# The rounds of an RWKV-7 scan: how TensorE waits, how it turns 64x64 blocks, and in which order four engines take their steps

## Chip, cores and metric

One core of a Trainium2 chip runs the whole program. The metric is the device time of one execution in microseconds (us). Engines are named PE (TensorE), ACT (ScalarE), DVE (VectorE), POOL (GpSimd) and SP (SyncE).

## The reference

Two blocks of a network run one after the other on 256 tokens (and 256 context tokens) of width 1024. The change touches one piece of the first block, the RWKV-7 scan with 16 heads of 64:

```
# rwkv7_scan: S (heads, 64, 64), one step for each token
sa = S @ (-kk_t)
S  = S * w_t + outer(sa, kk_t * a_t) + outer(v_t, k_t)
y_t = S @ r_t
```

It runs forward and backward in time. In each direction the context's tokens are scanned from a zero state, where only the last state is of use, and then the 256 latent tokens, whose outputs y are read.

## The kernel before

`rwkv_scan_stage` computes the scan in chunks of 64 tokens. The two directions are two **lanes**, 0 and 1, with tiles of their own. A **round** takes one chunk for 8 of the 16 heads, in both lanes. There are 16 rounds: 0 to 7 only write the state (`RW_READS` is 8), 8 to 15 also read outputs. In a round each lane solves a 64x64 triangular system for each head by doubling, in six levels. All of it is fp32. A product of 64x64 blocks is one call and two matmul records in the trace, so a step of 8 calls is 16 records ("x16").

The steps, with the lines that issue them on PE:

- `CT`, `LK` (`cross`, L3241, 16 records each) and `CC` (`cross_both`, L3250, moving 128 columns): the tables of the next round, from alpha, beta, kappa and the state. In read rounds `RKB` (L3241, 32 records) makes two tables with rho.
- `Y2` to `Y6` and `E2` to `E6` (`cross_late`, L3258, 16 records each): the levels. `D1` to `D5` turn the matrix `e` for them. In rounds 0 to 7 a turn is a product with the identity inside 64x64 tiles of the array (`turn_by_product`, L3241, 16 records); in rounds 8 to 15 it is two 128x128 transposes (`turn`, L3269, 2 records).
- `V` and `KB` turn v, kappa and beta, by 128x128 transposes in every round (2 and 4 records).
- `U`, `LKV`, `R` (`own`, L3264, 16 records), `S` and `O` (`cross` of two products, 32 records): update, state and outputs. A `'` in the order means the step of the round before, a `+` one of the round after.

One level of one lane is a chain over three engines: `Y` and `D` on PE, ACT copies both out of PSUM (L3384, L3391), `E` on PE, and DVE merges it into `e` (L3489), which the next `Y` reads.

`rwkv_order` gives each engine its own list of steps for a round. PE's instructions stand in two loops (`Fori`), of 8 and of 7 passes; round 15 stands behind them, unrolled. The other engines' instructions are unrolled. Since PE's loop body is the same in each pass, it waits against a register that grows by one in each pass, and adds one to a second semaphore:

```
def wait(e, lane, step):                                  # L3280
    pe.wait_ge(sig.sems[e, lane, step].sem, at)
    if not isinstance(at, int):
        pe.sem_inc(carried.sem, 1)
```

PE's order in rounds 0 to 7 is Y2 D1 U' of both lanes, E2 S', Y3 D2, V KB, E3 LKV, Y4 D3, E4, Y5 D4, E5, each for lane 0 and then lane 1; then Y6 D5 CT+ CC+ LK+ of lane 0, the same of lane 1, E6 E6. Rounds 8 to 15 add R behind D1, O' behind S' and RKB behind D3.

Of the kernel before, what the change touches and what calls it, by code (L numbers as in the profile page):

```python
# [3029 lines left out]

def rwkv_order(engine, n):

    late, read, more = n >= 1, n >= RW_READS, n + 1 < RW_ROUNDS
    inside = 0 <= n < RW_ROUNDS

    def lane(d, *steps):  # L3040
        at = {"'": n - 1, "+": n + 1}
        return [(d, s.rstrip("'+"), at.get(s[-1], n)) for s in steps]

    def both(*steps):
        return [x for d in LANES for x in lane(d, *steps)]

    fore = [lane(d, "CT+", "CC+", "LK+") if more else [] for d in LANES]
    reads, behind, kept = ["RKB"] * read, ["O'"] if n > RW_READS else [], ["S'"] if more else []
    if engine == "pe":
        if n < 0:  # L3050
            return fore[0] + fore[1]
        if read:
            behind = ["O'"]
        if not inside:
            return both("U'", *behind)
        return [*both("Y2", "D1", *["R"] * read, "U'"), *both("E2", *kept, *behind), *both("Y3", "D2"), *both("V", "KB"), *both("E3", "LKV"), *both("Y4", "D3", *reads), *both("E4"),
                *both("Y5", "D4"), *both("E5"), *lane(0, "Y6", "D5"), *fore[0], *lane(1, "Y6", "D5"), *fore[1], *both("E6")]
    if engine == "act":
        scales = both("shrink+", "grow+") if more else []
        if n < 0:  # L3060
            return scales
        behind = ["U'"]
        if not inside:
            return both(*behind)
        return [*both("Y2", "D1", *behind), *scales, *both("Y3", "D2"), *both("KB"), *both("Y4", "D3"), *both("Y5", "D4"), *both("Y6", "D5")]
    if engine == "dve":
        last = lane(0, "last+") + lane(1, "last+") if more else []
        if n < 0:
            return fore[0] + fore[1] + last
        if not inside:  # L3070
            return both(*behind)
        return [*both("copy"), *both("E2", *kept, *behind), *both("E3", "LKV"), *both(*reads), *both("E4"), *both("E5"), *fore[0], *fore[1], *both("E6"), *last]
    if n == RW_ROUNDS:
        return []
    ahead = [*both("ident+"), *both("alpha+"), *(both("scale'") if late and more else []), *both("state+", "vn+"), *both("beta+", "kappa+")] if more else []
    return [*ahead, *(both("rho+") if more and n + 1 >= RW_READS else []), *both(*["R"] * (read and inside))]


class ScanSignals:
# [3 lines left out]
    LAG = {"U": 1, "S": 1, "O": 1, "E6": 1, "kappa": -1}  # L3083
    STEPS = {"act": ("D1", "D2", "D3", "D4", "D5", "U", "KB", "grow", "shrink"),
             "dve": ("CC", "LK", "E2", "E3", "E4", "E5", "E6", "S", "O", "LKV", "RKB", "last", "copy"),
             "pool": ("alpha", "kappa", "rho", "scale", "R")}

    def __init__(self, core):
        self.sems = {(e, lane, s): core.counter(f"rw_{e}_{s}_{lane}") for e, steps in self.STEPS.items() for lane in LANES for s in steps}
        self.level = max(c.base for c in self.sems.values()) + 1  # L3090
        self.pe = [core.counter(f"rw_pe_steps_{lane}") for lane in LANES]
        self.pe_at, self.pe_n = {}, 0
        for n in range(-1, RW_ROUNDS + 1):
            for d, step, m in rwkv_order("pe", n):
                if d == 0:
                    self.pe_n += 1
                    self.pe_at[step, m] = self.pe_n

    def value(self, step, m):
        return self.level + m + 1 + self.LAG.get(step, 0)  # L3100

    def first(self, step):
        return RW_READS if step in ("R", "RKB", "rho", "O") else -1 if step in ("U", "S") else 0

    def align(self, eng):

        for (e, lane, s), c in self.sems.items():
            by = self.value(s, self.first(s) - 1) - c.base
            if by:
                eng.sem_inc(c.sem, by)  # L3110

    def wait_pe(self, eng, lane, step, m):
        eng.wait_ge(self.pe[lane].sem, self.pe[lane].at(self.pe_at[step, m]))

    def wait(self, eng, e, lane, step, m):
        eng.wait_ge(self.sems[e, lane, step].sem, self.value(step, m))

    def done(self, ins, e, lane, step, m):
        if (e, lane, step) not in self.sems:
            return  # L3120
        c = self.sems[e, lane, step]
        ins.then_inc(c.sem, 1)
        c.n = self.value(step, m) - c.base

    def settle(self):
        for c in self.pe:
            c.n += self.pe_n


def rwkv_scan_stage(core, st, rw):  # L3130
# [12 lines left out]
    with ExitStack() as ctx, core.engines_block() as block:  # L3143
# [16 lines left out]
        names = ("shrink", "kappa", "alpha", "rho", "e1", "e", "y", "d", "lk", "w", "vn", "store0", "store1")  # L3160
# [3 lines left out]
        for d in LANES:  # L3164
            sources, turned, rkb = (host[:, d * share + a * N * C:d * share + b * N * C].rearrange("p (x n t) -> p x n t", n=N, t=C) for a, b in ((0, 2), (2, 5), (5, 7)))
            cw = core.sb(f"cw_{d}", [P, N, 2, C], ctx=ctx)[:]
            ur = core.sb(f"ur_{d}", [P, 2, N, C], ctx=ctx)[:]
# [2134 lines left out]
```

## Time and profile before

| what | us |
|---|---|
| median of 3 runs | 3288.19 (3282.24 to 3291.73) |
| profiled execution | 3287.64, its span 3285.9 |
| scan stage, from POOL's first memset to the next stage's first matmul | 1056.2 to 1395.2 of the span |
| PE busy over the span | 3040.2 (93%) |
| mean granted clock of PE | 0.957 of 2.4 GHz |

The span runs from the first to the last instruction; the profiled execution's time is 1.7 us longer than it. Times in the rows are microseconds from the start of the span. Rows of one engine in a timeline overlap because matmuls are pipelined and their ends are modelled, so the cost of a step in a stream is the distance from its start to the start of the next. "PEclk" is the share of 2.4 GHz that PE was granted, and a row with "issue" is idle time in which PE waited for nothing that the profile shows.

### The profile page before, as it was taken

How to read it: one execution, taken by the hardware profiler on the slowest of the kernel's cores; microseconds unless marked ns; L12 is line 12 of the kernel's file. 1: busy time of each engine (PE TensorE's matmuls, PEld its weight loads, DVE VectorE, ACT ScalarE, POOL GpSimd, SP SyncE). 2: the span in 40 equal slices, each digit the busy share in tenths (PEclk: the TensorE clock that was granted, in tenths of full speed). 3: DMA queues.
4: the chain of work that ended last, by engine and by line, in shares of the span. 5: the costliest groups of instructions: out<-in, count | busy, mean ns of one | idle time of the engine just before them, and what ended most of it. 6: DMA issues, size and time to landing. Idle time of an engine off the chain costs nothing. (4 is left out here: it accounts for less than half of the span.)

```text
span 3285.9 us, 68297 instructions
## 1 busy us (share of the span) xinstructions
PE 3040.2 (93%) x27176; PEld 2492.1 (76%) x27176; DVE 2371.4 (72%) x3483; ACT 1743.1 (53%) x2797; POOL 615.4 (19%) x720
## 2 busy tenths in 40 slices
PE   5998889999797888879999999998999999999998
PEld 4774568878673777759986998866788888888887
DVE  5868754468847444477866778545799999999998
ACT  2424433232314443335445534765788888888887
POOL 0007124321100434318423111331000000000000
PEclk8998999999898999989989999998999999999999
DMA  6536224446211000048652798402899999999997
GB/s 221 170 108 20 103 84 153 141 147 207 96 58 26 1 1 1 2 171 271 253 161 65 275 328 302 140 27 79 320 370 367 371 369 366 373 366 368 370 360 261
DMA packets 337306, 646.56 MB, mean 197 GB/s; under 512 B 23853, under 2 KB 144281, under 8 KB 337113
## 3 DMA queue, kind: packets, MB, share of 16 engines
q1 hardware_dynamic: 316233, 568.38, 51.0%
q0 software_dynamic: 20160, 73.41, 6.1%
q8 instruction: 117, 1.92, 0.2%
q10 hardware_dynamic: 720, 2.23, 0.2%
q14 instruction: 76, 0.62, 0.1%
HBM read 641.34 MB, written 1.05 MB: 196 GB/s over the span
## 5 line engine op out<-in xcount | busy, mean ns | idle before, releaser
L5095 DVE TENSOR_TENSOR weights_lo<-raw_ring,weights_hi 128x1024 fp32r<-128x1024 f32 x336 | 400.8, 1220 | 35.6 <-ACT weights_hi L5025 28.4
L5025 ACT ACTIVATE weights_hi<-raw_ring 128x1024 fp32r<-128x1024 f32 x336 | 356.7, 1065 | 89.4 <-PE bank_pair L4961 53.2
L5095 DVE TENSOR_TENSOR weights_lo<-H,weights_hi 128x1024 fp32r<-128x1024 f32 x224 | 268.6, 1221 | 25.1 <-ACT weights_hi L5025 18.2
L4961 PE MATMUL bank_pair<-weights_hi,expert_x_hi 128*128 128x512 f32 x896 | 281.7, 396 | 4.9 <-DVE weights_lo L5095 4.8
L4961 PE MATMUL bank_pair<-weights_hi,expert_x_lo 128*128 128x512 f32 x896 | 277.2, 391 | 0.0
L4961 PE MATMUL bank_pair<-weights_lo,expert_x_hi 128*128 128x512 f32 x896 | 276.8, 390 | 0.0
L5025 ACT ACTIVATE weights_hi<-H 128x1024 fp32r<-128x1024 f32 x224 | 236.5, 1060 | 58.5 <-PE bank_pair L4961 43.2
L2715 DVE SCALAR_TENSOR_TENSOR conv<-bank_pair,vec,conv 128x189 f32<-128x189 f32 (+3 forms) x396 | 138.5, 427 | 146.0 <-ACT conv L2675 146.0
L4961 PEld LDWEIGHTS bank_pair<-weights_lo,expert_x_hi 128*128 128x128 f32 x896 | 168.5, 188 | 36.1
L4961 PEld LDWEIGHTS bank_pair<-weights_hi,expert_x_lo 128*128 128x128 f32 x896 | 168.5, 188 | 36.0
L4961 PEld LDWEIGHTS bank_pair<-weights_hi,expert_x_hi 128*128 128x128 f32 x896 | 163.8, 189 | 36.2 <-issue 5.1
L1349 PE MATMUL bank_pair<-Y_parts,const_parts 128*128 128x256 f32 (+1 forms) x592 | 145.7, 331 | 1.6 <-DVE H_parts L1394 1.6
L4973 PE MATMUL bank_pair<-weights_hi,hidden_hi 128*128 128x512 f32 x448 | 138.7, 391 | 0.0
L4973 PE MATMUL bank_pair<-weights_hi,hidden_lo 128*128 128x512 f32 x448 | 138.0, 389 | 0.0
L4973 PE MATMUL bank_pair<-weights_lo,hidden_hi 128*128 128x512 f32 x448 | 138.0, 389 | 0.0
L5095 DVE TENSOR_TENSOR weights_lo<-const,weights_hi 128x1024 fp32r<-128x1024 f32 x112 | 134.0, 1219 | 3.5
L5025 ACT ACTIVATE weights_hi<-const 128x1024 fp32r<-128x1024 f32 x112 | 119.4, 1066 | 31.9 <-PE bank_pair L4961 21.6
L629 DVE SCALAR_TENSOR_TENSOR mod_sums_ada<-mod_ring_ada,act,mod_sums_ada 128x1024 f32<-128x1024 f32 x84 | 115.4, 1379 | 4.8 <-DMA mod_ring_ada<-in_w_ada 4.8
L1349 PEld LDWEIGHTS bank_pair<-Y_parts,const_parts 128*128 128x128 f32 x592 | 101.9, 191 | 14.0 <-DVE const_parts L1329 2.4
L1138 PE MATMUL bank_pair<-const 128*128 128x512 f32 (+1 forms) x140 | 75.3, 649 | 32.2 <-PEq L214 32.2
L3384 ACT ACTIVATE const<-bank_pair 128x128 f32<-128x128 f32 x80 | 22.5, 282 | 150.3 <-PE bank_pair L3269 80.7
L1349 PE MATMUL bank_pair<-H_parts,const_parts 128*128 128x256 f32 (+1 forms) x296 | 97.7, 330 | 0.0
(802 smaller groups left out, 8366.9 us busy)
## 6 DMA issues: line engine op xcount, KB each, us to landing
raw_ring<-in_moe_w_gate SPq DMA_DIRECT2D x64, 1024.0 KB, 6.2
raw_ring<-in_moe_w_up SPq DMA_DIRECT2D x56, 1024.0 KB, 7.0
ring_up<-in_ffn_w_up SPq DMA_DIRECT2D x110, 512.0 KB, 4.0
H<-in_moe_w_down SPq DMA_DIRECT2D x48, 1024.0 KB, 5.1
raw_ring<-in_moe_w_down SPq DMA_DIRECT2D x48, 1024.0 KB, 5.1
mod_ring_ada<-in_w_ada POOLq DMA_DIRECT2D x84, 512.0 KB, 6.3
ring_down<-in_ffn_w_down SPq DMA_DIRECT2D x66, 512.0 KB, 6.0
H<-in_moe_w_gate SPq DMA_DIRECT2D x32, 1024.0 KB, 7.2
```

What stands on the lines that cost most here:

```text
L629: ins = self.core.nc.vector.scalar_tensor_tensor(total, tile, scale, total, ALU.mult, ALU.add)
L1138: core.nc.tensor.matmul(core.bank(bank)[:, cols], st.C("ones"), st.const[:, cols], start=True, stop=True)
L1349: ins = self.core.nc.tensor.matmul(self.bank(it, o)[:, 0:T], w, y, start=s == self.begin[o] and k == 0 and a == 0, stop=s == self.end[o] a ...
L2715: ins = nc.vector.scalar_tensor_tensor(out, shifted, tap(w, 2 * it + o), out, ALU.mult, ALU.add)
L3384: nc.scalar.activation(by_slot(t["y"])[:, :, :, 0:C // 2], Y[d], ACT.Copy)
L4961: ins = nc.tensor.matmul(bank, x[:, k * SEATS:(k + 1) * SEATS].bitcast(F32R), w[:, j * WIDE:(j + 1) * WIDE], start=k == 0 and i == 0, stop ...
L4973: ins = nc.tensor.matmul(DOWN[half], x, w[:, half * 512:(half + 1) * 512], start=c == 0 and i == 0, stop=c == FEC - 1 and i == 2)
L5025: nc.scalar.activation(hi[:, u % CUTS].bitcast(F32R), raw_part(u), ACT.Copy).then_inc(cut.sem, 1)
L5095: nc.vector.tensor_tensor(lo[:, u % CUTS].bitcast(F32R), raw_part(u), hi[:, u % CUTS], ALU.subtract).then_inc(parted.sem, 1)
```

## The change

1. **Waits.** Most semaphores that PE waits for become tokens: the producer adds one, PE waits for the constant 1 (`take`), and the second call of the step takes one away again (`then_inc(..., -1)`). Only `V`'s wait for `S` keeps its register. Six steps of a round (`Y2`, `CT`, `CC` of both lanes) take two tokens.
2. **Turns.** A turn is made inside 64x64 tiles: for s = 0 a transpose, for s = 1 a product with the identity, 12 records by the count of calls. It is used for D1 to D5 in every round, and for V and KB in rounds 0 to 7. In rounds 8 to 15 V and KB keep the 128x128 transposes.
3. **Tables.** alpha and rho stand side by side (`keys`), and `CT` and `LK` are `cross_both` products with both, 128 moving columns each, in every round; `RKB` goes. DVE masks the rho halves with two instructions (`RB`, `RK`) into `fresh`, and copies both to `rkb` later (`cp`).
4. **Order.** Lists written out by hand for four engines, one for write and one for read rounds.

```diff
+RW_STEPS = {
+    ("pe", False): "Y20 U0' D10 Y21 U1' D11 E20 S0' S1' E21 Y30 V0 D20 KB0 Y31 D21 E30 V1 KB1 E31 Y40 D30 LKV0 Y41 D31 LKV1 E40 E41 CT0+ Y50 D40 LK0+ Y51 D41 E50 CT1+ LK1+ E51 Y60 D50 CC0+ Y61 D51 E60 CC1+ E61",
+    ("act", False): "grow0+ shrink0+ U0' D10 U1' D11 grow1+ shrink1+ D20 D21 KB0 KB1 D30 D31 D40 D41 D50 D51",
+    ("dve", False): "copy1 copy0 E20 S0' E21 S1' E30 E31 LKV0 E40 last0+ last1+ E41 LKV1 CT0+ E50 LK0+ E51 CT1+ LK1+ CC0+ E60 CC1+ E61",
+    ("pool", False): "alpha0+ alpha1+ scale1' vn0+ beta0+ scale0' ident0+ kappa0+ vn1+ state1+ beta1+ ident1+ kappa1+ state0+",
+    ("pe", True): "Y20 R0 D10 U0' Y21 D11 R1 E20 U1' E21 S0' O0' S1' Y30 D20 Y31 O1' D21 E30 V0 KB0 V1 KB1 E31 LKV0 Y40 D30 Y41 D31 LKV1 E40 CT0+ E41 LK0+ Y50 D40 Y51 D41 CT1+ E50 LK1+ E51 Y60 D50 CC0+ Y61 D51 E60 E61 CC1+",
+    ("act", True): "grow0+ D10 U0' D11 shrink0+ U1' grow1+ shrink1+ D20 D21 KB0 KB1 D30 D31 D40 D41 D50 D51",
+    ("dve", True): "copy1 copy0 E21 E20 O0' S0' O1' S1' E30 E31 last0+ LKV0 cp0 LKV1 E40 cp1 E41 CT0+ RB0+ LK0+ RK0+ E50 CT1+ E51 RB1+ LK1+ RK1+ CC0+ E60 E61 last1+ CC1+",
+    ("pool", True): "R0 alpha1+ alpha0+ rho1+ scale0' rho0+ beta0+ beta1+ ident0+ kappa0+ vn0+ state0+ ident1+ kappa1+ scale1' vn1+ R1 state1+",
+}
...
+    def take(self, eng, e, lane, step):
+        c = self.tokens[e, lane, step]
+        eng.wait_ge(c.sem, c.base + 1)
+        return c.sem
...
-            def turn_by_product(out, x):
-                return cross(out, [(x, ident)])
+            def turn(out, x):
+                for j in (0, 1):
+                    for s in (0, 1):
+                        for r in (0, 1):
+                            head, unit = x[HALF[r], 2 * j + s], st.C("pair_ident")[HALF[r]]
+                            if s:
+                                ins = nc.tensor.matmul(out[HALF[s], r, j], head, unit, start=True, stop=True)
+                            else:
+                                ins = nc.tensor.transpose(out[HALF[s], r, j], head, unit)
+                return ins
...
+                    def first(ins):
+                        count[0] += 1
+                        if count[0] > 1 and taken:
+                            ins.then_inc(taken.pop(0), -1)
...
                     if step == "CT":
-                        wait("pool", d, "kappa")
+                        take("pool", "kappa")
                         if n >= 0:
-                            wait("dve", d, "RKB" if n >= RW_READS else "LKV")
-                        ins = cross(SLOT0[d], [(t["beta"], t["alpha"])])
+                            take("dve", "LKV")
+                        ins = cross_both(WIDE0[d], t["beta"], t["keys"], first)
+                    elif step == "LK":
+                        ins = cross_both(WIDE1[d], t["kappa"], t["keys"], first)
                     elif step == "CC":
-                        ins = cross_both(WIDE[d], t["alpha"], t["sources"])
+                        take("pool", "state")
+                        take("dve", "LK")
+                        ins = cross_both(WIDE1[d], t["alpha"], t["sources"], first)
...
                     elif kind == "D":
-                        ins = (turn if n >= RW_READS else turn_by_product)(TURN[d], t["e1" if l == 1 else "e"])
+                        ins = turn(TURN[d], t["e1" if l == 1 else "e"])
...
-                        cross(SLOT0[d], [(t["kappa"], t["rho"])])
-                        ins = cross(SLOT1[d], [(t["beta"], t["rho"])])
...
                     elif step == "R":
-                        sig.wait(pool, "act", d, "U", m - 1)
+                        sig.wait_pe(pool, d, "O", m - 1)
...
+                    elif step in ("RB", "RK"):
+                        mask = st.C(f"upto_{d}").unsqueeze(1).unsqueeze(1).to_broadcast([P, 2, 2, C])
+                        if m > RW_READS:
+                            sig.wait(dve, "dve", d, "cp", m - 1)
+                        wide_slot, i = (WIDE0, 1) if step == "RB" else (WIDE1, 0)
+                        ins = nc.vector.tensor_tensor(by_slot(t["fresh"][:, i]), wide_slot[d][:, :, :, 1], mask, ALU.mult)
+                    elif step == "cp":
+                        ins = nc.vector.tensor_copy(t["rkb"], t["fresh"])
```

## Rows read from the trace of the kernel before

**Rows 1.** The windows view, seven rounds of the scan: length, busy time of each engine, granted clock
```profile
1065.60:1086.70 21.10, 16.55 (x732) 14.93 (x724) 8.48 (x25) 8.03 (x28) 6.13 (x12) 1.00 0.02 4
1137.80:1154.90 17.10, 14.96 (x719) 14.03 (x716) 8.17 (x26) 8.05 (x28) 7.20 (x14) 1.00 0.00 0
1206.20:1236.10 29.90, 24.61 (x736) 21.34 (x736) 9.72 (x28) 8.71 (x28) 9.94 (x18) 0.77 0.01 3
1236.10:1258.80 22.70, 20.59 (x736) 18.06 (x736) 9.60 (x29) 8.67 (x28) 9.90 (x18) 0.92 0.00 0
1280.50:1302.20 21.70, 19.19 (x740) 16.81 (x736) 10.05 (x30) 8.67 (x28) 9.89 (x18) 1.00 0.00 1
1302.20:1326.80 24.60, 22.10 (x740) 19.34 (x736) 10.02 (x29) 8.71 (x28) 9.90 (x18) 0.86 0.00 0
1348.50:1371.60 23.10, 20.59 (x740) 18.04 (x736) 10.00 (x29) 8.66 (x28) 9.90 (x18) 0.93 0.00 0
```

**Rows 2.** The view of TensorE's register waits, line 3280, over the span
```profile
L3280 PEldq EVENT_SEMAPHORE  x552: 51/51/51, 1065.1 to 1371.0; - x184
```

**Rows 3.** The timeline of TensorE in one write round: start, length, group, idle before it
```profile
1139.33 0.43 PE L3258 MATMUL bank_pair<-const,cw 64*64 64x32 f32 x16 [1.49 <-DVE const L3489]
...
1149.12 0.43 PE L3258 MATMUL bank_pair<-const,cw 64*64 64x32 f32 x16
1149.34 0.47 PE L3241 MATMUL bank_pair<-const 64*64 64x64 f32 x16
1149.60 0.42 PE L3258 MATMUL bank_pair<-Y,cw 64*64 64x32 f32 x16
...
1150.48 0.44 PE L3258 MATMUL bank_pair<-const 64*64 64x32 f32 x16 [0.20 <-ACT const L3391]
...
1151.46 0.43 PE L3258 MATMUL bank_pair<-const,cw 64*64 64x32 f32 x16
...
1151.94 0.44 PE L3241 MATMUL bank_pair<-const,H 64*64 64x64 f32 x16
1152.17 0.65 PE L3250 MATMUL bank_pair<-H,const 64*64 64x128 f32 x16
1152.61 0.44 PE L3241 MATMUL bank_pair<-const 64*64 64x64 f32 x16
```

**Rows 4.** The timeline of TensorE in one read round
```profile
1282.39 0.44 PE L3269 MATMUL bank_pair<-const 128*128 128x128 f32 x2
1282.76 0.68 PE L3264 MATMUL bank_pair<-const,H 64*64 64x64 f32 x16
1283.28 0.57 PE L3264 MATMUL bank_pair<-const 64*64 64x64 f32 x13
...
1283.71 0.41 PE L3258 MATMUL bank_pair<-Y,cw 64*64 64x32 f32 x14
...
1290.13 0.38 PE L3269 MATMUL bank_pair<-const,H 128*128 128x128 f32 x2
1290.45 0.43 PE L3258 MATMUL bank_pair<-const 64*64 64x32 f32 x16
```

**Rows 5.** The timeline of ScalarE and TensorE: a register wait released, write round
```profile
1147.66 0.30 ACT L3391 ACTIVATE const<-bank_pair 128x128 f32<-128x128 f32 x1
...
1148.10 0.43 PE L3258 MATMUL bank_pair<-const 64*64 64x32 f32 x16 [0.20 <-ACT const L3391]
```

**Rows 6.** The same in the last round, which waits on a constant
```profile
1387.95 0.27 ACT L3391 ACTIVATE H<-bank_pair 128x128 f32<-128x128 f32 x1
...
1388.28 0.43 PE L3258 MATMUL bank_pair<-Y,H 64*64 64x32 f32 x16 [0.17 <-ACT H L3391]
```

**Rows 7.** The timeline of TensorE in the expert stage: four transposes and what follows
```profile
2585.14 0.60 PE L4932 MATMUL bank_pair<-const 128*128 128x128 f32 x4
2585.50 0.71 PE L4961 MATMUL bank_pair<-weights_hi,expert_x_hi 128*128 128x512 f32 x2
```

**Rows 8.** Groups by line and shape, VectorE in the scan stage: busy, mean ns, idle before
```profile
L3507 DVE TENSOR_TENSOR H<-bank_pair,const 128x512 f32<-128x512 f32 x16 | 11.1, 691 | 12.2 <-PE bank_pair L3241 12.2
```

More of the change, by code:

```diff
@@ L3028 @@
 LANES = (0, 1)
-def rwkv_order(engine, n):
[L3037 to L3076, printed above, removed]
@@ new lines @@
+RW_STEPS = {
[8 rows of a table added]
+}
+def rwkv_order(engine, n):
+    read, more = n >= RW_READS, n + 1 < RW_ROUNDS
+    steps = []
+    for word in RW_STEPS[engine, read].split():
+        step, d, at = step_of(word)
+        ahead, behind = at == "+", at == "'"
+        if (ahead and not more) or (not ahead and n < 0) or (not behind and n == RW_ROUNDS):
+            continue
+        if (step == "S" and not more) or (step == "scale" and not (n >= 1 and more)) or (step == "O" and engine == "dve" and n == RW_READS):
+            continue
+        first_read = n == RW_READS - 1
+        if first_read and engine == "pool" and step == "kappa":
+            steps.append((d, "rho", n + 1))
+        steps.append((d, step, n + ahead - behind))
+        if first_read and engine == "dve" and step in ("CT", "LK"):
+            steps.append((d, "RB" if step == "CT" else "RK", n + 1))
+    return steps
@@ L3079, with step_of @@
+def step_of(word):
+    at = word[-1] if word[-1] in "+'" else ""
+    word = word.rstrip("+'")
+    return word[:-1], int(word[-1]), at
 class ScanSignals:
[L3083 to L3086, printed above, removed]
+    STEPS = {"act": ("grow", "shrink"), "dve": ("S", "O", "last", "copy", "CT", "cp"), "pool": ("scale", "R")}
+    TOKENS = {"act": ("D1", "D2", "D3", "D4", "D5", "U", "KB"), "dve": ("E2", "E3", "E4", "E5", "E6", "LKV", "LK", "CC"), "pool": ("kappa", "state")}
@@ L3112, in wait_pe @@
[L3112 to L3127, printed above, removed]
+                self.pe_n[d] += 1
@@ L3159, in tile @@
             return t.rearrange("p (n t) -> p n t", n=N)
-        names = ("shrink", "kappa", "alpha", "rho", "e1", "e", "y", "d", "lk", "w", "vn", "store0", "store1")
+        names = ("shrink", "kappa", "e1", "e", "y", "d", "lk", "w", "vn", "store0", "store1")
         T = [{n: tile(f"{n}_{d}") for n in names} for d in LANES]
@@ L3232, in _, with cross @@
         def _(pe):
-            ident = st.C("pair_ident").unsqueeze(1).to_broadcast([P, N, C])
-            def cross(out, products):
+            def cross(out, products, first=lambda ins: None):
                 for j in (0, 1):
@@ new lines, in rounds_from @@
+                            if not isinstance(at, int):
+                                pe.sem_inc(carried.sem, 1)
+                                carried.n += times
+                        else:
+                            pe.wait_ge(sig.sems["dve", d, "O"].sem, sig.value("dve", d, "O", n - 1))
+                        ins = (turn_whole if n >= RW_READS else turn)(SLOT2[d], t["vn"])
+                    elif step == "KB":
+                        by = turn_whole if n >= RW_READS else turn
+                        by(SLOT0[d], t["kappa"])
+                        ins = by(SLOT1[d], t["beta"])
+                    else:
+                        take("act", "KB")
+                        ins = own(SLOT0[d], t["lk"], t["vt"], first)
```

164 lines of the change are left out of this document (81 added, 83 removed).

## The prediction

> **What bounds the kernel now.** I read the page first: PE is busy 93% of the span, but the change touches one stage of 339 us, so only that stretch counts. Then the windows view by rounds, where the reader is to see four things. A write round takes 17.1 us at the full clock and a read round 21.7. Rounds 9, 12 and 14 are read rounds too and take 22.7, 24.6 and 23.1, with granted clocks of 0.92, 0.86 and 0.93; round 8 takes 29.9 at 0.77. Round 0 takes 21.1 at full clock. DVE, ACT and POOL stay at or under 10.1 of 21.7 us [rows 1]. So PE's sequence sets the length, as busy time and as waits for a chain that comes back to PE. Next the timeline of PE. Each pass of a loop starts with 1.49 us of idle PE. In a level without other work, level 5 of lane 0 starts at 1149.12 and level 6 at 1151.46: 2.34 us, while PE's six steps in between need 1.4, and the gap stands ahead of E5, which waits for ACT [rows 3]. PE executes 552 register waits of 51 ns each, some 37 in a pass [rows 2].
>
> **Prices of the steps on PE**, start to start. Y .22 ahead of a turn (I take .21 for Y and E); a turn by products .26; CT .23, CC with 128 moving columns .44 [rows 3]. R is .52 behind a 128x128 turn, U .43, so .47 for an own step; S and O are two crosses, .47. A 128x128 turn takes .37, and Y in front of it another .36 to .37 in place of .22, so going in and out of the full array costs some .25 a turn. Two full transposes with the way out cost .32 [rows 4], four without one .36 [rows 7]; so the 12 of V and KB are 1.1 to 1.3, with .3 for in and out.
> Write round before: 20 Y and E 4.2, 10 D 2.6, six own or double steps 2.8, V and KB 1.6, CT and LK .95, CC .9: 13.05. Add 1.49 idle and .2 for refilling PE at the loop's head; the other 2.35 are waits of the levels' chains. Read round before: 4.2, D 3.7 and 1.5 for the changes, ten own or double steps 4.7, V and KB 1.6, CT, LK, RKB and CC 2.8: 18.5. With the head 1.7 that leaves 1.5 of waits.
>
> **The edits.**
> *Turns.* A new turn has 12 records against 16 of the product. Nearest rows: 12/16 of CT's .23, that is .17, from below; above, a full turn with its changes of tile each time, .51. The two tiles that hold products still issue as many records each as in CT, so I take .24. V and KB in write rounds are six such turns, 1.45 against 1.6. The open question is whether a transpose among products empties the array. In the expert stage four transposes stand between products in one tile shape: start to start .36 for the four, under .1 each, so nothing is paid between the last of them and the product behind it [rows 7]. The cost in [rows 4] then belongs to the change of tile, which the new turn never makes. The Trainium skill says the same of the change (TensorEngine Tiling (Array Packing), Tiling Modes: changing the tiling mode drains the engine). It also speaks against this edit: by its Restrictions, column tiling excludes transpose mode for fp32. By the rows the turn is .24 or less; by that rule it would be a product, .26, some .3 us more in a round.
> *Tables.* CT and LK rise from .23 to .44. In write rounds this is work for nothing: 4 x .21 = +.84. In read rounds it replaces RKB: 4 x .44 against 4 x .23 and two times .47, -.1. DVE's masks go from 2 x .69 to more, smaller ones, and `cp` is new: a copy of 128x512, between nothing and the .69 of a mask of that size [rows 8]. DVE then has about 11.5 of 18 us, so it is covered by PE.
> *Waits.* A register wait released by ACT at 1147.96 lets PE start at 1148.10, .14 later [rows 3, 5]. In the last round, which waits on constants, ACT ends at 1388.22 and PE starts at 1388.28: .06 [rows 6]. So .08 for each exposed wait, and one event less at the loop's head, .15 by two such waits. The 34 taken tokens in a round each add a decrement to a matmul; no row shows its price, bounded by 0 and the 51 ns of an event [rows 2]. I take 0: a step that ends in an increment is followed at the same distance as any.
> *Order.* In levels 4 to 6 CT, LK and CC of both lanes now stand between E and Y, or Y and E. A level has .84 for Y and D of both lanes, .42 for E and .88 of tables, 2.2 in all, against a chain of 2.34 that loses two waits of .08 and is 2.2. PE is then bound by its own steps, and of 2.4 us of waits I keep .4. What is late next is POOL. In read rounds R0, which waits for O0', heads its list, and alpha, rho, beta and kappa for the next round are queued behind it. O0' ends about 4.1 us into the round; POOL's instructions take 9.89/18 = .55 [rows 1], kappa0 is the tenth and ends at 9.6; CT0 comes up at 10.1 on PE. This is .5 us of cover; I keep .8 of waits in a read round.
> *Prologue.* Two more memsets and another order on POOL: between 0 and 1 us, I take +1. The loops stay, so the head's idle time and round 0's extra do.
>
> **Sum.** Write round after: Y, E 4.2; D 2.4; own and double 2.8; V, KB 1.45; tables 6 x .44 = 2.65; head 1.55; waits .4: 15.45, so -1.65. Read round: 4.2, 2.4, 4.7, V and KB still on the full array 1.6, 2.65, 1.55, .8 = 17.9; against 21.7 I take -3.7. Eight of each: -13 and -29 (the last read round has no tables and gains less). The falls of the clock cost 1.0 + 2.9 + 1.4 in rounds 9, 12 and 14, and 5.2 in round 8 once 3 us of stalls of its first pass are taken off, 10.5 in all. They come only where D is a full turn [rows 1]; I take half back, -5. In all -13 - 29 - 5 + 1 = -46. The profiled execution took 3287.64 and the median is 0.55 above it, so both lead to 3242.
>
> **Rivals.**
> A, the other side: the transpose inside 64x64 tiles empties the array as a full turn does, .51 a turn. Sixteen turns in a write round and ten in a read round, 208 in all, at +.27: +56, so 3298. It decides from .46 a turn. For it: every full turn next to a 64x64 step pays. Against it: [rows 7]. .07.
> B: the clock also falls in write rounds. Transposes stand near all falls of the scan and products near none. A fall of one granted stretch costs 1.0 to 1.4; one in each round is +20 against the forecast: 3262. .12. The Trainium skill has such a rule (TensorE: Matmul & The Clock Gate, Part 4: transposes do not count as work for the clock in the same way).
> C: POOL is late. If the chain behind R0 ends 2 us later than I work out, CT0 stands for 1.5 in each read round: +12, 3254. .10.
> D: the decrements are not free. At 26 ns, half of an event's 51, 34 in a round are .9 us: +14, 3256. .06. The Trainium skill gives 26.3 ns for each increment that serializes (TensorE: Matmul & The Clock Gate, Part 3), which is near that half.
> E: the waits don't shrink, because the order only moves them, so that only the turns, the tables and a third of the clock come through: write rounds gain nothing, read rounds 2.5 each, -20 -3.5 +1: 3265. .07.
> My forecast has .58.
>
> **Range and chances.** 3228 to 3266. The low end is all of the clock back (-5.5), no waits in a round (-9): 3227. The high end takes in B to E one at a time. Faster by over 0.3% (9.9 us, about what a measurement here can tell from no change): forecast, B, C, D and E, less what an unknown stall could take: .88. Within 0.3%: .05, slower .07, nearly all from A.
>
> **What would show it.** Windows over a write round 15.2 to 15.7 long with PE idle only at its head, 1.3 to 1.4 us; a read round 17.5 to 18.5. D's start to the next step's .22 to .26 in all rounds; over .4 is A. A row with PE waiting for POOL's kappa is C. A granted clock of 1.00 in write rounds and above 0.95 in rounds 8 to 14; below that is B. Steps of 16 records at more than .22 with no wait named are D. The forecast is wrong if the level's period in the write rounds stays at 2.3.

## The result, and the profile after

The changed kernel took 3355.28 us (median of 4 runs, 3335.48 to 3357.55), the kernel before 3289.96 (4 runs beside it, 3282.24 to 3295.8): ratio 1.0187, interval 1.0142 to 1.0231. It is slower. The forecast was 3242 with a range of 3228 to 3266, so both the sign and the range were wrong.

The profiled execution took 3355.53 us. Its scan stage runs from 1056.1 to 1463.3 us of the span, 407.2 us in place of 339.0: the stage holds the whole difference. Up to the first branch of the loop (start of the stage and round 0) it takes 40.5 us in place of 30.1; rounds 1 to 7 together 181.6 in place of 119.5; rounds 8 to 14 160.5 in place of 165.5; the last one 24.6 in place of 23.8. So the write rounds lose 62 us, round 0 10, and the read rounds gain 5.

The windows view of the kernel after, one round to a row but for the last row (columns as in [rows 1]): write rounds 2 and 3, read rounds 10 and 11, and then the half-clock stretch inside round 2.

```profile
1121.10:1150.70 29.60, 29.39 (x747) 23.95 (x744) 8.23 (x24) 8.27 (x30) 7.11 (x14) 0.77 0.00 0
1150.70:1175.20 24.50, 24.30 (x748) 20.03 (x748) 8.16 (x25) 8.31 (x30) 7.06 (x14) 1.00 0.00 0
1324.10:1347.00 22.90, 22.56 (x785) 19.64 (x781) 11.31 (x32) 8.62 (x28) 10.02 (x18) 1.00 0.00 0
1347.00:1370.00 23.00, 22.66 (x787) 19.71 (x783) 11.34 (x33) 8.62 (x28) 10.02 (x18) 1.00 0.00 1
...
1130.30:1144.00 13.70, 13.70 (x238) 10.91 (x238) 2.22 (x8) 2.89 (x8) 4.75 (x10) 0.50 0.00 1
```

Read the first number against PE's busy time. In the write round of 24.5 us PE is busy for 24.3; in [rows 1] it was 14.96 of 17.10. The waits are gone, as the change meant, and yet the round is 7.4 us longer, with hardly more matmul records (748 against 719). More time for the same number of records is the signature of a dearer record, not of a wait. The first row adds a second, smaller loss: 13.7 us at a granted clock of 0.50, 1.2 GHz, make one round 5.1 us longer. There are three such stretches, in rounds 0, 2 and 6: some 15 us together, if the one in round 0 costs as much as the other two.

The view of waits says the same of the whole stage (us in total, times, longest). First the kernel before, PE over 1056 to 1395 us, then the kernel after, 1056 to 1463:

```profile
PE bank_pair L3258 <- DVE const L3489: 27.6, 23, 1.5
PE bank_pair L3241 <- POOL const L3419: 10.9, 1, 10.9
```

```profile
PE bank_pair L3248 <- POOL const L3425: 9.9, 1, 9.9
PE bank_pair L3257 <- ACT Y L3397: 3.1, 9, 0.3
PE bank_pair L3257 <- issue: 1.7, 8, 0.2
PE bank_pair L3257 <- DVE const L3494: 0.8, 2, 0.5
```

27.6 us of waits for VectorE's merge became .8. The largest wait left is that for POOL at the stage's start, which both have.

Where the time went is in the timeline of PE in a write round of the kernel after. L3281 is the new turn's transpose, L3279 its product; the cost of a step is again the distance to the next start.

```profile
1187.12 0.25 PE L3281 MATMUL bank_pair<-const,H 64*64 64x64 f32 x2
1187.29 0.33 PE L3279 MATMUL bank_pair<-const,H 64*64 64x64 f32 x4
1187.56 0.25 PE L3281 MATMUL bank_pair<-const,H 64*64 64x64 f32 x2
1187.73 0.27 PE L3279 MATMUL bank_pair<-const,H 64*64 64x64 f32 x2
...
1188.43 0.25 PE L3281 MATMUL bank_pair<-const 64*64 64x64 f32 x2
1188.61 0.33 PE L3279 MATMUL bank_pair<-const 64*64 64x64 f32 x4
1188.87 0.24 PE L3281 MATMUL bank_pair<-const 64*64 64x64 f32 x2
1189.05 0.28 PE L3279 MATMUL bank_pair<-const 64*64 64x64 f32 x2
```

Two transposes take .17 to .18, the two products behind them (x4) .26 to .27, and this twice: .88 us a turn, against .24 in the forecast and .26 for a turn by products [rows 3]. The four products of a turn all write the same half of the tiles, that is two tiles of the four. An `own` step also uses two tiles only, and its 16 records take .43 to .52 [rows 4] where those of a cross, in four tiles, take .23 [rows 3]. By that measure four records in two tiles cost some .12; here they cost .26. The tile shape (64*64) never changes. A passage between transpose and product, in either direction, seems to cost some .15, and the new turn makes four of them, since its innermost loops put two transposes, two products, two transposes, two products in a row. That was the theory that the experiments had to test.

### The profile page after: what moved, and what is told of

It is laid out like the page before. It is cut to its first block and busy times, and to the rows that moved or that the text cites. A ratio compares the mean times of both kernels' runs of the same rounds, so it can differ in the third digit from the quotient of the medians.

```text
span 3353.8 us, 68802 instructions
## 1 busy us (share of the span) xinstructions
PE 3141.5 (94%) x27624; PEld 2560.0 (76%) x27624; DVE 2381.7 (71%) x3517; ACT 1747.5 (52%) x2797; POOL 613.1 (18%) x720
## 5 line engine op out<-in xcount | busy, mean ns | idle before, releaser
L5107 DVE TENSOR_TENSOR weights_lo<-H,weights_hi 128x1024 fp32r<-128x1024 f32 x224 | 268.9, 1223 | 24.9 <-ACT weights_hi L5037 18.2
L4985 PEld LDWEIGHTS bank_pair<-weights_lo,hidden_hi 128*128 128x128 f32 x448 | 84.1, 188 | 17.6
```

The source lines that it names most:

```text
L4985: ins = nc.tensor.matmul(DOWN[half], x, w[:, half * 512:(half + 1) * 512], start=c == 0 and i == 0, stop=c == FEC - 1 and i == 2)
L5107: nc.vector.tensor_tensor(lo[:, u % CUTS].bitcast(F32R), raw_part(u), hi[:, u % CUTS], ALU.subtract).then_inc(parted.sem, 1)
```

## The experiments

Theory P: the passages between transposes and products cost the time, four a turn. Rivals: S, the transposes or the new layout cost it wherever they stand; and that the other parts of the change (order, tokens, tables) carry some of it. `twice`, `padded`, `updates`, `events`, `narrow`, `shifted64` and `short_shifted` were executed once each, so they are read by the rounds of their one trace and their whole times are only rough.

**1. Turns by products alone (`products`).** The changed kernel, with one edit:

```diff
-    if s:
-        ins = nc.tensor.matmul(out[HALF[s], r, j], head, unit, start=True, stop=True)
-    else:
-        ins = nc.tensor.transpose(out[HALF[s], r, j], head, unit)
+    ins = nc.tensor.matmul(out[HALF[s], r, j], head, unit, start=True, stop=True)
```

> The changed kernel with its turn made of eight products with the identity and no transpose, all else as it is. In the changed kernel's trace a turn takes .88 us, in four pieces: two transposes .18, four records of products .26, and the same again; the product turn of the kernel before took .26. Theory M (each passage between transposes and products inside 64x64 tiles costs some .15 us, four in a turn): 208 turns at -.62 us, -129 us, so 3226, and a write round falls from 24.5 to about 14.6 us, a read round from 22.9 to 16.7. Rival R (the new order, the tokens or the wider tables are what made the kernel slower): 3340 or more. If the falls of the clock in rounds 0, 2 and 6 (5.1 us each) go too, 3211.

Measured: 3266.78 us, ratio 0.9931 (0.9907 to 0.9955). Write rounds take 14.5 us as expected, read rounds 17.1, but every second read round takes 29 to 30.5 and the first 23.3, and so the whole missed the 3226 that was expected. Its windows, one write and three read rounds:

```profile
1112.20:1126.70 14.50, 14.29 (x813) 14.02 (x812) 8.78 (x25) 7.84 (x30) 6.99 (x14) 1.00 0.00 1
1208.20:1225.30 17.10, 16.46 (x819) 15.89 (x817) 11.04 (x32) 8.49 (x28) 9.97 (x18) 1.00 0.00 1
1225.30:1254.30 29.00, 20.69 (x826) 19.39 (x822) 10.95 (x33) 8.67 (x28) 9.99 (x18) 0.82 0.02 5
1254.30:1271.40 17.10, 16.46 (x818) 15.88 (x815) 11.03 (x32) 8.48 (x28) 9.96 (x18) 1.00 0.00 1
```

24.47 less 14.47 is 10.0 us for 16 turns, .62 each, and .88 - .26 is .62. The write rounds are explained by the turns alone. The long read rounds were no part of any theory; see 5.

**2. The same twelve calls in another order (`grouped`).** The loops over j and s change places, so that four transposes stand together and then four products:

```diff
-    for j in (0, 1):
-        for s in (0, 1):
+    for s in (0, 1):
+        for j in (0, 1):
             for r in (0, 1):
```

> The changed kernel with the loops of the turn changed in order alone: the four transposes first, then the four products. Same records, two passages in a turn in place of four. Theory M (a price for each passage): .15 to .17 less for each passage saved, a turn of .55, 208 turns at -.33: -69 us, 3286. Rival S (a transpose of fp32 in a 64x64 tile is slow by itself, whatever stands beside it): .88 a turn and 3355 again.

Measured: 3289.35 us, ratio 1.0003 (0.9984 to 1.0022); both kinds of round 20.2 us, no fall of the clock in them. The same work, two passages a turn fewer, and 4.3 us less in a write round: 32 passages, .13 each. P holds; S, as the sole cause, falls.

**3. Twice the transposes, no more passages (`twice`).** As `grouped`, with `for s in (0, 0, 1)`: the four transposes are made twice.

> As `grouped` (four transposes, then four products in a turn; 20.2 us a write round, against 14.5 with products alone: .36 more for each of 16 turns), but the four transposes are done twice over in each turn. Theory P (each passage between transpose and product costs, some .15, and a transpose beside a transpose .03 to .05): 20.2 + 16 x .12 to .2 = 22.1 to 23.4 us. Rival Q (a transpose itself costs .1 or more inside 64x64 tiles, however it is placed): 16 x .4 more, 26 us or more. With three passages fewer than the changed kernel's turn it would by P still be shorter than its 24.5.

Measured: 22.0 us a write round, at the low edge of P's range; 1.8 more than `grouped`, .11 for four transposes more. (The whole took 3348.23; four of its read rounds are long, see 6.) The timelines of PE, a turn of `grouped` and then one of `twice`:

```profile
1154.89 0.30 PE L3281 MATMUL bank_pair<-const,Y 64*64 64x64 f32 x4
1155.12 0.45 PE L3279 MATMUL bank_pair<-const,Y 64*64 64x64 f32 x8
```

```profile
1156.27 0.41 PE L3281 MATMUL bank_pair<-const,Y 64*64 64x64 f32 x8
1156.61 0.28 PE L3279 MATMUL bank_pair<-const,Y 64*64 64x64 f32 x2
```

Two transposes last .17 to .18 to the next start, four .23, eight .34. That is a line: .028 for each transpose and .12 that does not grow. The transpose is as cheap as a product's record in two tiles (.03); the passage is the price. On the products' side, `grouped` has .38 for eight records (1155.12 to the next transposes at 1155.50), where two tiles would take some .24: .14 more. A turn is then .24 + 4 x .028 and some .13 for each passage: .87 with four, .61 with two, against .88 measured and .62 from the rounds.

**4. The new turn in the kernel before, and the product turn there.** `before_mixed` puts the new turn, and `before_products` the turn by products, in the place of the kernel before's turns of D. In the read rounds ScalarE's copy and the next step follow the other layout; all else is as it was:

```diff
-    ins = (turn if n >= RW_READS else turn_by_product)(TURN[d], ...)
+    ins = turn_mixed(TURN[d], ...)          # before_products: turn_by_product
```

> The kernel before with the new turn (transposes for s = 0, products for s = 1) in D1 to D5 of every round, and nothing else changed: V and KB, waits, tables and order stay. Theory M: a turn of .88 lies in the chain of each level, +.62 against the product in write rounds and +.26 against a full turn with its changes of tile in read rounds; 10 turns a round: +6 and +2.6 us a round, +69 in all, 3357. If other parts of the change are what costs: 3275 to 3300.

> The kernel before with the product turn for D1 to D5 in read rounds too, and nothing else changed. Each of the ten turns of a read round falls from .62 (full turn with the change of tile on both sides) to .26. Theory: -3.6 us of PE work, of which some 2.5 come through because the chains of the levels take part of it, 8 rounds: -20; and the falls of the clock in rounds 8, 9, 12 and 14 lessen, -5 to -10: 3260. Rival: the falls of the clock have nothing to do with the full transposes; then they stay and it is 3268.

Measured: `before_mixed` 3432.11 (2 runs), ratio 1.043 (1.0401 to 1.046); `before_products` 3325.46, ratio 1.0101 (1.0078 to 1.0125). Write rounds of `before_mixed` take 22.5 us, 5.4 more than before for ten turns, .54 each; four of the seven from round 1 on have 6.8 us or more at half clock and take 25.4 to 26.5. The mechanism doesn't need the new order. Both times missed the expectation upward, for one reason above all: read rounds of 37 to 38 us in the one and, in four of six behind the first, 34 to 35 in the other (the other two take 19.8, where some 19.2 was expected).

**5. The long read rounds: instructions fetched again.** In a long round of `products` the timeline of PE has holes that nothing ends:

```profile
1276.18 0.65 PE L3257 MATMUL bank_pair<-const,cw 64*64 64x32 f32 x16 [4.20 <-issue]
1278.84 0.80 PE L3264 MATMUL bank_pair<-keys,H 64*64 64x64 f32 x10 [1.80 <-issue]
1286.02 0.40 PE L3278 MATMUL bank_pair<-const 64*64 64x64 f32 x12 [0.51 <-issue]
```

and the DMA view of 1221 to 1250, which holds most of the long round, shows one queue alone at work:

```profile
DMA packets 8, 0.13 MB, mean 5 GB/s; under 512 B 0, under 2 KB 0, under 8 KB 0
...
q8 instruction: 8, 0.13, 1.9%
```

Packets of 16 KB of instructions, one every 3.4 to 3.8 us. Short rounds have none or one, at their end. Counting PE's recorded instructions in a pass of the loop, a weight load for each matmul record included: before 1469 and 1515, after 1483 and 1555, `products` 1611 (write) and 1639 (read; 1631 in its short rounds and 1635 in `padded` and `shifted`, since a few records are missing from a trace), `before_mixed` 1715 and `before_products` some 1800 in read rounds. Behind the first pass of a loop, only the last three stall. The theory (F): a body above some 1611 to 1639 isn't held from one pass to the next. Two tests, `short` taking four turns by products out of the read loop's body (full transposes stand in their place), and `padded` putting two more into that of the write loop:

```diff
+def whole(n, l):
+    return n >= RW_READS and l >= 4
...
-    ins = turn(TURN[d], t["e1" if l == 1 else "e"])
+    ins = (turn_whole if whole(n, l) else turn)(TURN[d], t["e1" if l == 1 else "e"])
```

```diff
+    if l == 1 and n < RW_READS:
+        turn(TURN[d], t["e1"])
     ins = turn(TURN[d], t["e1" if l == 1 else "e"])
```

> The changed kernel with all turns inside 64x64 tiles as products (as in the run `products`), except that in the read rounds the turns D4 and D5 of both lanes are full 128x128 transposes again, with one full copy on ScalarE at the change of layout. This takes 4 x 12 = 48 records out of TensorE's loop body of the read rounds: 1639 become about 1591. Theory F (a loop body above some 1611 to 1639 TensorE instructions isn't kept from one pass to the next, and is fetched again): no pass but the first of the loop stalls; read rounds are 17.15 + 4 x .24 + about .1 = 18.2 us each, the four of 28.9 to 30.5 us go; write rounds stay at 14.5; the stage is about 278 us in place of 321.8, the kernel about 3225. Rival G (the long read rounds of `products` come from something else, such as the clock or a collision with DMA traffic): alternate read rounds stay at 28 to 30 us, the kernel stays at 3267 or more.

> As `products`, but in the write rounds D1 of both lanes is done twice over (the same eight products into the same place): 32 more TensorE records in the loop body of the write rounds, 1611 become 1643; the work is 2 x .26 = .5 us. Theory F: the write rounds, which took 14.5 us, stall for instructions in every or every second pass, 25 us or more where they do, with packets of the instruction queue in them. Rival G: 15.0 us in all of them. Read rounds as in `products`, 17.15 and 28 to 30 by turns.

Measured: `short` 3232.51 us, ratio 0.9839 (0.9809 to 0.987): write rounds 14.5, read rounds 18.0 from the second pass on, the stage 285.0. `padded` 3289.09: write rounds of 30.5, 30.9 and 28.9 us by turns with 15.0. The expectations counted matmul records alone; with the loads a turn by products is 32 instructions, so the body of `short` is 1523 and that of `padded` 1675. Windows of `short`, a write and a read round, and of `padded`, two write rounds and a read round:

```profile
1116.40:1130.90 14.50, 14.30 (x816) 14.02 (x811) 8.78 (x25) 7.85 (x30) 7.00 (x14) 1.00 0.00 1
1210.40:1228.50 18.10, 17.64 (x767) 16.22 (x764) 11.19 (x32) 8.69 (x28) 9.99 (x18) 1.00 0.00 0
```

```profile
1103.70:1134.20 30.50, 20.56 (x847) 19.72 (x843) 8.89 (x25) 8.52 (x30) 7.65 (x15) 0.78 0.02 5
1134.20:1149.20 15.00, 14.78 (x843) 14.51 (x838) 8.34 (x24) 7.72 (x28) 6.30 (x13) 1.00 0.00 1
1263.90:1281.10 17.20, 16.54 (x820) 15.90 (x817) 11.06 (x32) 8.48 (x28) 9.97 (x18) 1.00 0.00 0
```

Both bear F out in the main, but the short rounds of `padded` and its read loop do not fit it. That read loop is that of `products`, 1639 instructions, and none of its rounds behind the first stalls. So length isn't all.

**6. Length or place.** `shifted` is `products` with 32 semaphore instructions put once between the two loops of PE, `shifted64` with 64, `short_shifted` is `short` with 32:

```diff
+    if first == RW_READS:
+        for _ in range(32):
+            pe.sem_inc(carried.sem, 1)
+            carried.n += 1
```

> As `products` (all turns in 64x64 tiles are products), with 32 semaphore instructions put once between the write loop and the read loop of TensorE (32 x .05 = 1.6 us once). They move the read loop's body, 1639 instructions, by as many places as in `padded`, where the same body did not stall; the body itself is unchanged. If where the body starts decides whether it is kept between passes (fixed pieces, of which the body then takes up one less): all read rounds but the first 17.15 us, four long ones of 29 to 30.5 gone, 321.8 - 50 + 2 = 274 us for the stage, the kernel 3219. If the count in the body decides by itself, or if `padded` was luck: alternate rounds of 29 us as in `products`, 3268.

> As `shifted`, with 64 semaphore instructions between the loops in place of 32. In `products` (0) every second read round stalled for instructions, in `shifted` (32) each of them, in `padded` none, with the same body of some 1639. If the place of the body within fixed pieces decides, another place gives another pattern: none, every second or all. If the pattern at this length is not set by the place, every second again, 3270.

> As `short` (read loop's body 1591 by count, no stalls but in its first pass, rounds of 18.03), with the 32 semaphore instructions between the loops that made every read round of `shifted` stall. If the length decides first and the place only near the limit: 18.0 to 18.1 us in all read rounds but the first, the kernel 3234. If the place alone decides: rounds of 29 us or more.

Measured: `shifted` 3319.69, ratio 1.0109 (1.0091 to 1.0127), with all six read rounds behind the first at 30 to 32 us; `shifted64` 3235.58 with all six at 17.1, behind a first one of 32.9; `short_shifted` 3238.45 with all six at 18.2. A read round of each in that order, from their windows views:

```profile
1213.00:1244.40 31.40, 20.31 (x821) 19.00 (x817) 11.46 (x33) 8.69 (x28) 9.95 (x18) 0.84 0.02 5
```

```profile
1220.80:1237.90 17.10, 16.47 (x820) 15.85 (x816) 11.01 (x32) 8.48 (x28) 9.96 (x18) 1.00 0.00 1
```

```profile
1216.00:1234.20 18.20, 17.75 (x768) 16.30 (x764) 11.15 (x32) 8.68 (x28) 9.98 (x18) 1.00 0.00 0
```

The expectation for `shifted` fell, and by the same miscount: `padded` had moved the read loop by 64 instructions, not 32. `shifted64` is the run that puts it there again, and again no round stalls. So the same body of 1639 stalls every second time at its first place, always when it stands 32 instructions further on (`shifted`), and never at 64 (`padded` and `shifted64`). Length matters too: no body of 1611 or less stalled in a later pass, `short`'s 1523 at neither of its two places, while the 1675 of `padded` did every second time. Between these, a body of 1639 in the write rounds of `events` below did not.

Place and length together don't settle it either. `twice` has as many recorded instructions as `products` in both loops, and yet of its six read rounds behind the first the first and the last take 21.3 and 21.6 us, and the four between them 30.5 to 31.7. A short and a long one:

```profile
1264.00:1285.40 21.40, 21.06 (x826) 19.25 (x822) 11.27 (x32) 8.59 (x28) 10.05 (x18) 1.00 0.00 1
1315.90:1347.60 31.70, 25.13 (x824) 22.80 (x820) 11.29 (x32) 8.69 (x28) 10.06 (x18) 0.78 0.02 5
```

And two passes of some 1800 instructions in `before_products` ran in 19.8 us without one packet. The Trainium skill (Runtime: NRT & Kernel Launch, Instruction fetch mechanics) states 128 KiB, or 2048 instructions, for TensorE, refilled in blocks of 256. As an estimate by that figure, a body of 1639 lies in 7 or in 8 blocks by where it starts, and the buffer would have 8. That stalls begin at lengths near this agrees; but 8 or 9 packets came in each stalled pass, and which starts and which passes are bad was not worked out. The mechanism of the refetching stays open.

**7. The other parts, one at a time.** `updates` adds an increment and a decrement to two more calls of each step of products other than the turns, 64 in a write round. `events` adds a semaphore instruction of its own beside each token. `narrow` moves alpha's columns alone in the tables of the write rounds, and so leaves out the rho tables of the first read round. `before_head` is the kernel before with E6 of lane 0 ahead of lane 1's tables.

```diff
     if count[0] > 1 and taken:
         ins.then_inc(taken.pop(0), -1)
+    elif count[0] in (5, 6):                                  # updates
+        ins.then_inc(carried.sem, 1 if count[0] == 5 else -1)
...
     taken.append(sig.take(pe, e, d, step))
+    pe.sem_inc(carried.sem, 1)                                # events
...
+    if n < RW_READS:                                          # narrow; LK likewise
+        ins = cross(WIDE0[d][:, :, :, 0], [(t["beta"], t["alpha"])], first)
...
-    *fore[0], *lane(1, "Y6", "D5"), *fore[1], *both("E6")]    # before_head; DVE likewise
+    *fore[0], *lane(1, "Y6", "D5"), *lane(0, "E6"), *fore[1], *lane(1, "E6")]
```

> As `products`, but each step with taken tokens has two more semaphore updates on its fifth and sixth call (one up, one down, on a semaphore that nobody waits for): some 68 more in a round beside the 34 decrements. If an update costs nothing on TensorE (my recorded forecast): write rounds 14.5 us, as in `products`. Rival D (26 ns each): 16.2 us; the 34 decrements themselves then cost .9 us a round.

> As `products`, but each of the taken tokens is accompanied by a separate semaphore instruction on TensorE, as each wait was in the kernel before: 32 more in a write round, 51 ns each in the rows of before. If such instructions run ahead of the products (TensorE's sequencer has slack behind a full queue of products): write rounds at 14.5 to 14.8 us. If each takes its time on the path: 14.5 + 1.6 = 16.1. The loop body has 34 more instructions, so some passes may stall for instructions; the others are to be read.

> As `products`, but CT and LK of the write rounds move only alpha's 64 columns, as in the kernel before; the rho tables of the first read round (made in the last write round by the same loop body) are left out, so one round's outputs lack them. By my recorded term (4 x .21): write rounds 14.5 - .84 = 13.65 us. Rival: TensorE then waits for the levels' chain instead, and they stay above 14.2.

> The kernel before with one change of order: E6 of lane 0 comes ahead of lane 1's tables on TensorE and on VectorE. If the 1.49 us of idle TensorE at the loop's head is a wait for VectorE, which works through lane 1's masks before E60 (the reading after the result): write rounds fall from 17.1 to about 15.7 us and read rounds by 1 or more, the kernel about 3292 - 16 x 1.3 = 3271. If it is the loop's own (the recorded reading): both stay, 3290.

Measured, write rounds at the full clock: `updates` 14.5 us, as `products`, so a decrement on a product costs nothing to be seen. `events` 15.0, +.5 for 28 instructions of 51 ns: over a third of their time is on the path. (Its read rounds can't be read: every second one takes 32 to 33 us, and the others 19.2 or more with a fall of the clock in them.) `narrow` 14.1, -.34 in place of -.84. `before_head` 16.3 in place of 17.1 (15.7 was expected), read rounds 20.6 in place of 21.7, in all 3267.93, ratio 0.9948 (0.9924 to 0.9971). The timeline of PE at the head of a pass in `before_head`, where 1.49 us stood in [rows 3]:

```profile
1118.64 0.41 PE L3258 MATMUL bank_pair<-Y,H 64*64 64x32 f32 x16
1119.37 0.43 PE L3258 MATMUL bank_pair<-const,cw 64*64 64x32 f32 x16 [0.31 <-issue]
```

The idle head fell to .3, so 1.2 of it was VectorE's queue; of that 1.2, .8 came through in a write round. The times of `updates`, `events` and `narrow` as wholes (3267.26, 3286.83, 3269.91) hold the long read rounds of `products` too and say nothing more.

**8. The undo of the one part (`old_turns`).** The changed kernel with the turns of the kernel before: products for D in write rounds, full 128x128 transposes for D in read rounds (D's line is that of `short`) and for V and KB everywhere.

```diff
+def whole(n, l):
+    return n >= RW_READS
...
-    by = turn_whole if n >= RW_READS else turn
+    by = turn_whole                                           # V likewise
```

> The changed kernel with the turns of the kernel before: D in write rounds as products inside 64x64 tiles, D in read rounds and V and KB in all rounds as full 128x128 transposes. Waits, tables and the order of the four engines stay as changed. Theory P (the loss sits in the new turns alone): write rounds as in `products`, 14.5 to 14.9 us; read rounds 17.15 + 10 x (.5 - .26) = 19.5 at the full clock, with some falls of the clock as in the kernel before; no stalls for instructions, the body of the read rounds being some 1500; the stage about 290, the kernel 3237. Rival: order, tokens and wide tables are worth nothing without cheaper turns: 3285.

Measured: 3241.66 us (3240.12 to 3244.62), ratio 0.9871 (0.9855 to 0.9888). Its windows, a write and a read round:

```profile
1116.40:1131.70 15.30, 15.10 (x731) 14.23 (x730) 8.32 (x25) 8.01 (x30) 6.98 (x14) 1.00 0.00 1
1251.30:1270.50 19.20, 19.03 (x684) 16.41 (x680) 11.72 (x32) 8.66 (x28) 9.96 (x18) 1.00 0.00 1
```

Taken together, the other parts of the change gain time: without the new turns the kernel is faster than before by 1.3%, and with them slower by 1.9%. The rounds of `old_turns` have no fall of the clock, although the read rounds hold as many full transposes as those of [rows 1]. `short` is the fastest version that was run, 1.6% under the kernel before.

## Why the prediction was wrong

**The step that failed** is the price of the turn: "A new turn has 12 records against 16 of the product ... I take .24", with .51 as the upper bound. It measured .88. What the prediction left out is the passage between transposes and products inside 64x64 tiles, some .13 us each and four in a turn. The reason given, that in the expert stage "nothing is paid between the last of them and the product behind it [rows 7]", holds for that stage. The kernel before has the rows that say so, full transposes in a row in a write round, and the products around the four of [rows 7]:

```profile
1143.72 0.66 PE L3269 MATMUL bank_pair<-const 128*128 128x128 f32 x4
1144.21 0.38 PE L3269 MATMUL bank_pair<-const,H 128*128 128x128 f32 x2
1144.43 0.38 PE L3269 MATMUL bank_pair<-const,vn 128*128 128x128 f32 x2
...
2584.68 0.62 PE L4961 MATMUL bank_pair<-weights_lo,expert_x_hi 128*128 128x512 f32 x2
...
2586.05 0.63 PE L4961 MATMUL bank_pair<-weights_hi,expert_x_lo 128*128 128x512 f32 x2
```

In a row a full transpose costs .11 (.22 for two). In the expert stage a pair of products takes .46 (2584.68 to 2585.14), and the four transposes with the pair behind them .91 (2585.14 to 2586.05). That leaves .45, four times .11, and nothing for a passage. (The .36 of the prediction ends at the start of the next product and is short by what that product starts late.) The step from there to the new turn is what failed: a passage that is free between full transposes and products of 128x512 was taken to be free inside 64x64 tiles too. No row of the scan before has a transpose in such tiles. In [rows 4], where the price was .25 a turn, the tile shape and the kind of operation change together, and I put it down to the shape alone. So the bounds should have held a passage's price times the number of passages, four, and not one full turn. With .25 for a way in and out in the prediction's own terms, two ways in and out make .24 + 2 x .25 = .74 a turn and some 3346 us.

**Tiling modes.** I took support from the Trainium skill (TensorEngine Tiling (Array Packing), Tiling Modes), that a change of mode drains the engine. The runs show that some .12 to .16 is paid with no change of the tile; what the change of tile alone costs, no run shows. The same page's restriction against fp32 transposes with column tiling, which I weighed as .3 us a round, did not come about as a fall back to products: transposes ran, .028 us each.

**Rival A** named the mechanism and was given .07. Its price, .51, was the bound above, so it said 3298. With .88 it is 208 x .64 = 133 us over the forecast, 3375.

**Rival B** (the clock falls in write rounds) came true in part: three stretches, some 15 us against the 20 it named. My forecast had none in write rounds and half of those in read rounds gone; in the read rounds they are all gone. What decides was not settled: `grouped` and `old_turns` have many transposes and no fall in their rounds, `before_mixed` has one in four of seven write rounds, and a fall also stands in every refetched read round behind the first, in `products` as in `twice`.

**Order and waits** did more than forecast. "The loops stay, so the head's idle time and round 0's extra do" was a misreading: the row itself says that the idle time ended with VectorE's merge [rows 3], and I booked it as the loop's own. 7. shows that 1.2 of the 1.49 was VectorE working through lane 1's masks first. In write rounds `products` takes 14.5 where the forecast's terms, with .26 a turn, give 15.8; in read rounds 17.1 against 18.1. In 15 such rounds this is some -17 us.

**Tables**: +.84 was the price of the records, +.34 the effect. Where CT and LK stand, between the levels of a chain, part of their time fills waits that would otherwise be there.

**Tokens**: 0 for the decrements was right, and rival D (26 ns each) is out: 64 further updates in a write round changed it by less than .1 us (14.51 against 14.46). The Trainium skill gives 26.3 ns per increment (TensorE: Matmul & The Clock Gate, Part 3), for the tail behind packed products; it does not show on these streams of short products.

**Rivals C and E** did not occur: POOL's kappa is never waited for behind the stage's start, and the waits did shrink.

**The sum** then reads: 3242 + 133 for turns + 15 for the clock - 17 for order and head is 3373, against 3355. Of the 18 left, some 8 lie in the read rounds' losses of before, of which the forecast kept 3 us for stalls in round 8 and 5 for the clock: neither came, and round 8 takes 23.0 as the rounds behind it do. Some 3 more are waits in read rounds that the dearer turns took the place of (17.1 + 6.2 would be 23.3, measured 22.9). The rest was not placed.

That `old_turns` lands on 3242 is partly chance: it has dearer turns than forecast in read rounds, and gains more at the head.

## What to carry to other kernels

On TensorE, count the passages between transposes and products, not the transposes: group the transposes, or, for 64x64 blocks in fp32, turn by products, which cost .26 for eight among their like. Before a fixed price is blamed on one thing that changes in a row, look for a second thing that changes there, compare a group of two with a group of four to tell a fixed price from one per record, and don't carry a price of nothing from one tile shape to another. When a loop's body on TensorE is made longer than some 1600 instructions, loads included, look for "issue" holes and instruction packets in the later passes; a body that lies near the limit can fall on either side by where it starts.

## What the runs showed of the hardware that was not expected

- Inside 64x64 tiles, fp32: a transpose (one record) .028 us in a row of its like, a product (two records) .033 where four tiles share them and some .06 in two tiles, and some .12 to .16 more at each passage from one to the other. In the full array, between transposes and products of 128x512, a passage cost nothing: four transposes took .45, and .11 each in a longer row.
- TensorE's loop bodies of 1611 instructions and less passed without a stall for instructions after the first pass; one of 1639 fetched 8 or 9 packets of 16 KB in every pass, in every second or in none, by where it stood, and took 29 to 32 us in place of 17.1 where it did. The granted clock was 0.82 to 0.89 in these rounds of `products` and `shifted`. Passes of 1675 and some 1800 ran without a stall too, beside others that stalled.
- A decrement or increment attached to one of a stream of products costs nothing that shows; a semaphore instruction of its own cost some 18 ns of its 51 in the write rounds.
- The first pass of the read loop can be slowed in the same way: it brought 5 to 7 packets in every run, and took 21.3 us in `short` against 18.0 and 32.9 in `shifted64` against 17.1, but 23.0 against 22.9 in the changed kernel. Its longer rounds may hide the packets; no run tests that.
